# Seven block products in place of eight for four chunk pairs of two gated feed-forward stages

## The chip, the cores and the metric

The kernel runs on one core of one Trainium2 chip. The time is the device time of one execution in microseconds. Before the change it is 990.17 us, the median of three runs (990.16 to 990.27).

## The reference, cut to what matters

Two transformer blocks run on a 256 x 1024 activation `h` in float32. The first block has a gated feed-forward stage, a mixing stage with two kinds of attention, and a second gated feed-forward stage; the second block has attention beside a recurrence, and a squared feed-forward stage. The change touches the two gated stages:

```
def swiglu(x, w_gu, w_down):
    gate, up = jnp.split(x @ w_gu, 2, axis=-1)      # w_gu 1024 x 5632
    return (jax.nn.silu(gate) * up) @ w_down        # w_down 2816 x 1024

h = h + 0.5 * swiglu(rmsnorm(h, ffn1_norm), ffn1_w_gu, ffn1_w_down)
...
h = h + 0.5 * swiglu(rmsnorm(h, ffn2_norm), ffn2_w_gu, ffn2_w_down)
```

## The kernel before, in words

Every large product is made in three passes of fp32r operands. A 128 x 2048 block of weights (four K tiles by 512 columns, 1 MB, called a unit) is loaded by SyncE's queue into one of three buffers `raw`; ScalarE copies it to `hi` (`split_hi`), VectorE subtracts to get `lo` (`split_lo`), and TensorE computes x_hi w_hi + x_hi w_lo + x_lo w_hi. There are three `hi` and three `lo` buffers, so `split_hi` of unit n waits until TensorE has used unit n - 3 (`used` at least n - 2). `portion` is one unit against one tile of 128 tokens: 4 K tiles x 3 passes = 12 matmuls of 128x128 by 128x512. A plain unit is two portions, one for each token tile.

A gated stage is cut into 11 chunks of 256 hidden columns. A chunk's gate and up columns stand side by side in one 512-wide product, whose K = 1024 is two units, so that a chunk is 2 up-projection units (`ffn_up`) and one down-projection unit (`ffn_down`). The order on TensorE is up(i), down(i - 1), in a loop on each engine (`ffn_iter`). The product of chunk i and token tile t goes to PSUM bank `G[t]`. ScalarE takes silu of the left half (`ffn_act`), VectorE multiplies with the right half (`ffn_hidden`), and splits the result's 32-bit words in 16-bit planes (`halves`, `ffn_planes`). SyncE transposes these by DMA (`flip`), VectorE puts the words together (`ffn_merge`), and ScalarE and VectorE split them in `hh` and `hl` (`ffn_hi`, `ffn_lo`) for the down-projection. Its four PSUM banks `DB` gather all chunks. `up(i + 1)` may write `G[t]` only after `ffn_hidden(i, t)` has read it.

The squared stage at the end already has the technique that the change brings to the gated ones: for chunk pairs (2, 3) and (6, 7) the 2 x 2 block product of (two token tiles) by (two chunks) by (two halves of K), eight portions, is made by seven portions on sums of weight blocks (`weight_sum`, VectorE, 128x2048 each), and sums of activation blocks (`x_sums`, `sum_hi`, `sum_lo`, once per stage). Partial results go from PSUM to `xn` (`keep`, ScalarE; `add_product`, VectorE). A product there is a unit that is used by one portion only.

All orders are written out by hand, for each engine a list of calls; every engine works its list strictly in order and waits on counting semaphores. SyncE's queue does this with loads and transposes alike: a load that stands behind a transpose is issued after it.

Of the kernel before, what the change touches and what calls it, by code (L numbers as in the profile page):

```python
# [75 lines left out]

U_F1 = 0
U_M1 = U_F1 + 3 * NF1
U_B1 = U_M1 + 2 * len(IN1)
U_F2 = U_B1 + 8  # L80
U_M2 = U_F2 + 3 * NF1
# [4 lines left out]
PAIRS = (2, 6)  # L86


# [15 lines left out]
OPERAND = {"p1": 0, "p2": 1, "p6": 5, "p7": 2, "p5": 4, "p4": 1, "p3": 3}  # L104
LAST = last_order()
PLAIN = [i for i in range(NF2) if i // 2 * 2 not in PAIRS]
LAST_LOADED = [x for x in LAST if x[0] in "ud"]
UNITS = U_L + len(LAST)

# [6 lines left out]
def slot_of(kind, i, b):  # L116

    return U_L + LAST_LOADED.index((kind, i, b))


def slot_unit(r):

    return r if r < U_L else unit_of(*LAST_LOADED[r - U_L])
# [119 lines left out]
class GatedFfn(Ffn):  # L243


    def __init__(self, sem, name, base, norm, earlier=None):
        super().__init__(sem, name, base, NF1, norm)
        self.past = 0 if earlier is None else NF1
# [8 lines left out]
    def k_tiles(self, i):  # L257

        return 2 if isinstance(i, int) and i == self.chunks - 1 else 0

    def up_unit(self, i):
        return self.base + (0 if i == 0 else 2 + 3 * (i - 1))


class SquaredFfn(Ffn):


    def __init__(self, sem, name, base, norm):
        super().__init__(sem, name, base, NF2, norm)
        self.own(sem, name)  # L270
        self.b_in = [sem(f"{name}_b_in{j}") for j in range(4)]
        self.t_made = sem(name + "_t_made")
        self.s_made = sem(name + "_s_made")
        self.s_hi = sem(name + "_s_hi")
        self.s_lo = sem(name + "_s_lo")
        self.kept = sem(name + "_kept")
        self.added = sem(name + "_added")


def program(nc, a, out):  # L280
    ctx = ExitStack()
    with ctx:
# [40 lines left out]
        with scope() as s:  # L323

            hh = sb("hh", [P, 4, SEQ], F32R, s)
            hl = sb("hl", [P, 4, SEQ], F32R, s)
            halves = sb("halves", [P, NT, 2 * W], U16, s)
            halves_t = sb("halves_t", [P, 8, SEQ], U16, s)
            hid_t = sb("hid_t", [P, 4, SEQ], F32, s)

        with scope() as s:

            operand = {j: sb(f"operand{j}", [P, 4, W], F32, s) for j in (2, 1, 3, 4, 5)}
            sum_h = sb("sum_h", [P, 16, P], F32R, s)
            sum_l = sb("sum_l", [P, 16, P], F32R, s)
# [5 lines left out]
            operand[0] = sb("operand0", [P, 4, W], F32, s)  # L341
# [55 lines left out]

        def whole(n):

            kind, i, b = LAST[n - U_L]  # L400
            return operand[OPERAND[kind]] if kind in OPERAND else raw[slot_of(kind, i, b) % RING]
# [157 lines left out]

        ffns = [GatedFfn(sem, "f1", U_F1, 0)]  # L560
        ffns.append(GatedFfn(sem, "f2", U_F2, 2, ffns[0]))
# [26 lines left out]
        def _(sp_eng):  # L588
            def load(n, src, off=0, dst=None):
                s = n % RING  # L590
                if n >= RING or not isinstance(off, int):

                    sp_eng.wait_ge(lo_done, n - 2 + RING * off)
                sp_eng.dma_start(raw[s][:, :, :] if dst is None else dst(raw[s]), src).then_inc(raw_in[s], UNIT_IN)

            def gate_up(w, n, i, half, off=0):

                s = n % RING
                if n >= RING or not isinstance(off, int):
                    sp_eng.wait_ge(lo_done, n - 2 + RING * off)  # L600
                for g in range(2):
                    src = gu_view(w)[:, bass.ds(i, 1), 4 * half:4 * half + 4, g, :]
# [3 lines left out]
            def columns(w, n, first, half, off=0, width=W):  # L606
                load(n, col_view(w)[:, 4 * half:4 * half + 4, bass.ds(first, width)], off,
                     lambda t: t[:, :, 0:width])

            def down(w, n, i):  # L610
                load(n, down_view(w, 2)[:, i, :, :], 0,
                     lambda t: t[:, :, :].rearrange("p (k h) c -> p k (h c)", h=2))

            def flip(f, i):

                for t in range(NT):
                    sp_eng.wait_ge(f.planes, 2 * i + t + 1)
                    if i > 0:
                        sp_eng.wait_ge(f.merged, i)
                    sp_eng.dma_start_transpose(halves_t[:, 0:4, t * P:(t + 1) * P],  # L620
                                               halves[:, t, 0:W]).then_inc(f.flip[t], 16)

            def last_operand(j, b):

                half, chunk = b % 2, PAIRS[j] + b // 2
                if j == 0:
                    sp_eng.wait_ge(*((k_pv, NH), (k_rl, 2), (k_ri, 8), (k_rl, 2))[b])
                else:
                    sp_eng.wait_ge(lo_done, unit_of(("p1", "p4", "p7", "p3")[b], PAIRS[j - 1]) + 1)
                    sp_eng.wait_ge(last.t_made, 4 * j - (3, 0, 1, 1)[b])  # L630
                src = col_view(a["w_up_2"])[:, 4 * half:4 * half + 4, chunk * W:chunk * W + W]
                sp_eng.dma_start(operand[b][:, :, :], src).then_inc(last.b_in[b], 16)

            def last_load(kind, i, b):

                r = slot_of(kind, i, b)
                sp_eng.wait_ge(lo_done, slot_unit(r - RING) + 1)
                if kind == "u":
                    src = col_view(a["w_up_2"])[:, 4 * b:4 * b + 4, i * W:i * W + W]
                    dst = raw[r % RING][:, :, :]  # L640
                else:
                    src = down_view(a["w_down_2"], 4)[:, i, 2 * b:2 * b + 2, :]
                    dst = raw[r % RING][:, :, :].rearrange("p (k h) c -> p k (h c)", h=2)
                sp_eng.dma_start(dst, src).then_inc(raw_in[r % RING], UNIT_IN)
# [9 lines left out]
            def swiglu_weights(w_gu, w_down, f):  # L654
                gate_up(w_gu, f.base, 0, 0)
                gate_up(w_gu, f.base + 1, 0, 1)
                for i in range(1, NF1):
                    n = f.up_unit(i)
                    if i >= 3:
                        flip(f, i - 2)  # L660
                    gate_up(w_gu, n, i, 0)
                    if i == 2:
                        flip(f, 0)
                    gate_up(w_gu, n + 1, i, 1)
                    down(w_down, n + 2, i - 1)
                flip(f, NF1 - 2)
                down(w_down, f.base + 2 + 3 * (NF1 - 1), NF1 - 1)
# [7 lines left out]
            def slot(n, j):  # L675
# [10 lines left out]
            slot(0, 0)  # L686
            slot(0, 1)
            quarter(1)
            for j in range(2, 4):
                slot(0, j)  # L690
            quarter(2)
            slot(1, 0)
            quarter(3)
            for j in range(1, 4):
                slot(1, j)
            sp_eng.wait_ge(first_hi, 2)
            for j in range(4):
                slot(2, j)
# [13 lines left out]
            down(a["ffn1_w_down"], 4, 0)  # L712
# [10 lines left out]
            part = P // 8  # L723
            for i in range(2, NF1):
                n = ffns[0].up_unit(i)
                if i >= 3:
                    flip(ffns[0], i - 2)
                gate_up(a["ffn1_w_gu"], n, i, 0)
                if i == 2:
                    flip(ffns[0], 0)  # L730

                    sp_eng.wait_ge(ftab_done, 1)
                    sp_eng.wait_ge(pool_made, 1)
                gate_up(a["ffn1_w_gu"], n + 1, i, 1)
                if i < NF1 - 1:
                    sp_eng.dma_start(table[:, (i - 2) * part:(i - 1) * part, :],
                                     ftab[:, :].unsqueeze(1).to_broadcast([24, part, ROW])).then_inc(tab_out, 16)
                down(a["ffn1_w_down"], n + 2, i - 1)
            flip(ffns[0], NF1 - 2)
            down(a["ffn1_w_down"], U_M1 - 1, NF1 - 1)  # L740

# [5 lines left out]
            for c, (first, width, _) in enumerate(IN1):  # L747
                for half in range(2):
                    columns(a["w_in"], U_M1 + 2 * c + half, first, half, width=width)
# [29 lines left out]
            swiglu_weights(a["ffn2_w_gu"], a["ffn2_w_down"], ffns[1])  # L779
# [17 lines left out]
            for c, (first, _) in enumerate(IN2):  # L797
                for half in range(2):
                    if half == 1 and by_dma(c - 3):
                        flip_mixed(c - 3)  # L800
                    columns(a["w_in_2"], U_M2 + 2 * c + half, first, half)
                if c in (3, 6):
# [4 lines left out]
                if c == 12:  # L807
                    last_operand(0, 0)
                if c == 13:
                    last_operand(0, 2)  # L810
# [7 lines left out]
            for c in range(2):  # L818
                for half in range(2):
                    columns(a["w_out_2"], U_P2 + 8 + 2 * c + half, c * W, half)  # L820
                    if half == 1:
                        last_operand(0, (3, 1)[c])
# [12 lines left out]
            last_operand(1, 0)  # L835
# [3 lines left out]
            last_operand(1, 2)  # L839
            last_operand(1, 1)  # L840
            last_load("u", 4, 1)
            flip_last(2, 1)
            last_operand(1, 3)
# [120 lines left out]
        def _(act):  # L964
# [10 lines left out]
            def split_hi(n, off=0, width=W):  # L975
# [3 lines left out]
                act.wait_ge(raw_in[s], UNIT_IN * (n // RING + 1) + UNIT_IN * off)  # L979
                if n >= RING:  # L980

                    act.wait_ge(used, n - 2 + RING * off)
                nc.scalar.activation(hi[s][:, :, 0:width], raw[s][:, :, 0:width], ACT.Copy).then_inc(hi_done, 1)  # L983

            def split_hi_part(n, part):

                s = n % RING
                if part == 0:
                    act.wait_ge(raw_in[s], UNIT_IN * (n // RING + 1))
                    act.wait_ge(used, n - 2)  # L990
                cut = slice(2 * part, 2 * part + 2)
                ins = nc.scalar.activation(hi[s][:, cut, :], raw[s][:, cut, :], ACT.Copy)  # L992
# [1948 lines left out]
```

## Time and profile before

| | |
|---|---|
| median of the runs | 990.17 us |
| the profiled execution | 990.05 us, its span 988.0 us |
| TensorE busy | 981.1 us (99%) |
| VectorE busy | 705.7 us (71%) |
| ScalarE busy | 597.4 us (60%) |
| GpSimd busy | 120.7 us (12%) |
| TensorE's granted clock | full in all but the last slice |

The first gated stage runs from about 7 to 190 us, the second from about 385 to 573 us, and the squared one from about 812 us to the end. A share of busy time is a mean over all stages; for the change the stretch of the gated stages counts. TensorE's matmuls overlap, so a matmul's duration is longer than the distance from one start to the next; the distance is what counts in a row of them.

### The profile page before, as it was taken

The numbers are of one execution on the slowest core, as the hardware profiler recorded it, in microseconds if no ns is written. First come the engines' busy times: TensorE is split into PE (matmuls) and PEld (weight loads), VectorE is DVE, ScalarE is ACT, GpSimd is POOL, SyncE is SP. The second block draws the span as 40 slices with busy tenths as digits, with TensorE's granted clock in tenths as the row PEclk, the third lists the DMA queues.
The fourth block names the chain that finished last, engine by engine and source line by source line (L and its number), as shares of the span: only waits on it lengthen the run. The fifth ranks groups of instructions, "written<-read, shape, count | busy, mean of one in ns | idle before, by whom it ended". The sixth has DMA issues, their size and how long they took to land.

```text
span 988.0 us, 12498 instructions
## 1 busy us (share of the span) xinstructions
PE 981.1 (99%) x4576; PEld 805.1 (81%) x4576; DVE 705.7 (71%) x998; ACT 597.4 (60%) x809; POOL 120.7 (12%) x109
## 2 busy tenths in 40 slices
PE   8999999999999999999999999999999999999998
PEld 6788888888777788888888888888888888888887
DVE  5756565668987667665656677876689878977685
ACT  7344444577666636434444576868876548977772
POOL 0000000022300000000000031249923001000000
PEclk9999999999999999999999999999999999999999
DMA  8987776586544536657575578667665664695542
GB/s 261 284 264 263 229 257 215 170 310 194 167 129 157 184 128 219 214 174 249 170 249 173 188 224 245 176 192 173 217 227 188 238 214 150 201 315 176 188 111 95
DMA packets 167577, 201.96 MB, mean 204 GB/s; under 512 B 58081, under 2 KB 113770, under 8 KB 167402
## 3 DMA queue, kind: packets, MB, share of 16 engines
q1 hardware_dynamic: 166938, 201.21, 64.3%
q8 instruction: 28, 0.46, 0.2%
q10 hardware_dynamic: 592, 0.14, 0.1%
q14 instruction: 19, 0.16, 0.0%
HBM read 182.45 MB, written 5.77 MB: 190 GB/s over the span
## 4 chain that ended last, share of the span: by engine, by line
PE 96%; DVE 2%; ACT 1%; DMA 1%; issue 0%; POOL 0%; SPq 0%; ACTq 0%; DVEq 0%
PE bank L2380 23%; PE bank L2382 23%; PE bank L2381 23%; PE bank L2483 4%; PE bank L2482 4%; PE bank L2481 4%; PE bank L2602 3%; PE bank L2603 3%; PE bank L2601 3%; PE bank L2395 1%; PE bank L2637 1%; PE bank L2752 1%; DMA raw<-in_ffn_w_gu 1%; DVE lo L1626 0%; PE bank L2652 0%
## 5 line engine op out<-in xcount | busy, mean ns | idle before, releaser
L2380 PE MATMUL bank<-hi,xh 128*128 128x512 f32 (+1 forms) x904 | 359.1, 397 | 1.4 <-DVE lo L1981 1.3
L2382 PE MATMUL bank<-hi,xl 128*128 128x512 f32 (+1 forms) x904 | 351.6, 389 | 0.0
L2381 PE MATMUL bank<-lo,xh 128*128 128x512 f32 (+1 forms) x904 | 351.0, 388 | 0.0
L1609 DVE TENSOR_TENSOR lo<-raw,hi 128x2048 fp32r<-128x2048 f32 (+1 forms) x82 | 187.4, 2287 | 94.7 <-ACT hi L983 94.7
L983 ACT ACTIVATE hi<-raw 128x2048 fp32r<-128x2048 f32 (+1 forms) x85 | 161.1, 1898 | 90.9 <-PE bank L2483 57.4
L2380 PEld LDWEIGHTS bank<-hi,xh 128*128 128x128 f32 x904 | 169.8, 188 | 38.7 <-issue 2.1
L2382 PEld LDWEIGHTS bank<-hi,xl 128*128 128x128 f32 x904 | 169.7, 188 | 35.6
L2381 PEld LDWEIGHTS bank<-lo,xh 128*128 128x128 f32 x904 | 170.0, 188 | 32.8
L1626 DVE TENSOR_TENSOR lo<-raw,hi 128x1024 fp32r<-128x1024 f32 (+1 forms) x108 | 131.6, 1228 | 42.6 <-ACT hi L992 41.9
L992 ACT ACTIVATE hi<-raw 128x1024 fp32r<-128x1024 f32 x102 | 104.5, 1051 | 8.9 <-PE bank L2382 8.9
L2481 PE MATMUL bank<-hi,hh 128*128 128x512 f32 x176 | 69.1, 392 | 0.0
L2483 PE MATMUL bank<-hi,hl 128*128 128x512 f32 x176 | 68.6, 390 | 0.0
L2482 PE MATMUL bank<-lo,hh 128*128 128x512 f32 x176 | 68.5, 389 | 0.0
L1767 DVE TENSOR_TENSOR lo<-raw,hi 128x2048 fp32r<-128x2048 f32 x21 | 47.9, 2288 | 19.3 <-ACT hi L1118 19.3
L1051 ACT ACTIVATE act_out<-bank,small 128x256 f32<-128x256 f32 x44 | 20.8, 475 | 56.6 <-PE bank L2382 53.5
L899 POOL TENSOR_TENSOR small<-small 128x1 f32<-128x1 f32 x10 | 8.6, 864 | 371.1 <-DVE small L1633 351.8
L1058 ACT ACTIVATE hh<-hid_t 128x512 fp32r<-128x512 f32 x20 | 12.6, 632 | 66.0 <-DVE hid_t L1671 66.0
L2602 PE MATMUL bank<-lo,last_hh 128*128 128x512 f32 (+1 forms) x130 | 50.1, 386 | 0.0
L2603 PE MATMUL bank<-hi,last_hl 128*128 128x512 f32 (+1 forms) x130 | 50.1, 386 | 0.0
L2601 PE MATMUL bank<-hi,last_hh 128*128 128x512 f32 (+1 forms) x130 | 50.1, 386 | 0.0
L1118 ACT ACTIVATE hi<-raw 128x2048 fp32r<-128x2048 f32 x21 | 40.0, 1914 | 11.8 <-DMA raw<-in_w_down 4.6
L906 POOL TENSOR_TENSOR rstd_q<-ss_q,small 128x8 f32<-128x8 f32 x16 | 34.6, 2169 | 88.4 <-DVE ss_q L2058 88.2
(303 smaller groups left out, 1341.7 us busy)
## 6 DMA issues: line engine op xcount, KB each, us to landing
raw<-in_w_in SPq DMA_DIRECT2D x48, 1024.0 KB
raw<-in_ffn_w_gu SPq DMA_DIRECT2D x82, 512.0 KB
raw<-in_ffn_w_down SPq DMA_DIRECT2D x22, 1024.0 KB
raw<-in_w_down SPq DMA_DIRECT2D x16, 1024.0 KB
raw<-in_w_out SPq DMA_DIRECT2D x8, 1024.0 KB
operand<-in_w_up SPq DMA_DIRECT2D x8, 1024.0 KB, 7.2
raw<-in_w_up SPq DMA_DIRECT2D x8, 1024.0 KB
distance_table<-ftab SPq DMA_DIRECT2D x8, 576.0 KB
```

The costliest lines, as they stand in the source:

```text
L983: nc.scalar.activation(hi[s][:, :, 0:width], raw[s][:, :, 0:width], ACT.Copy).then_inc(hi_done, 1)
L992: ins = nc.scalar.activation(hi[s][:, cut, :], raw[s][:, cut, :], ACT.Copy)
L1609: nc.vector.tensor_tensor(lo[s][:, :, 0:width], raw[s][:, :, 0:width], hi[s][:, :, 0:width].bitcast(F32), ALU.subtract).then_inc(lo_done, 1)
L1626: ins = nc.vector.tensor_tensor(lo[s][:, cut, 0:width], raw[s][:, cut, 0:width], hi[s][:, cut, 0:width].bitcast(F32), ALU.subtract)
L2380: nc.tensor.matmul(o, sh, wh, start=first and j == 0, stop=False, skip_group_check=onto)
L2381: nc.tensor.matmul(o, sh, wl, start=False, stop=False, skip_group_check=onto)
L2382: ins = nc.tensor.matmul(o, sl, wh, start=False, stop=last and j == 3, skip_group_check=onto)
L2481: nc.tensor.matmul(dst, sh, wh, start=first and k == 0, stop=False)
L2482: nc.tensor.matmul(dst, sh, wl, start=False, stop=False)
L2483: ins = nc.tensor.matmul(dst, sl, wh, start=False, stop=end)
L2601: nc.tensor.matmul(dst, sh, wh, start=begin, stop=False)
L2602: nc.tensor.matmul(dst, sh, wl, start=False, stop=False)
```

## The change

In both gated stages the chunks 4 and 5, and 8 and 9, are made by the seven products p1 to p7. The sequence of units of a stage is now a list:

```
FIRST_PAIRS = ((4, 8), (4, 8))
def gated_order(pairs):
    order = [("u", i, u) for i in range(2) for u in range(2)]
    for i in range(2, NF1 - 1, 2):
        d = [("d", i - 2 + c, 0) for c in range(2)]
        if i in pairs:
            p = {k: (k, i, 0) for k in OPERAND}
            order += [p["p1"], p["p2"], p["p6"], d[0], p["p7"], p["p5"], d[1], p["p4"], p["p3"]]
        else:
            order += [("u", i, 0), ("u", i, 1), d[0], ("u", i + 1, 0), ("u", i + 1, 1), d[1]]
    i = NF1 - 1
    return order + [("u", i, 0), ("u", i, 1), ("d", i - 2, 0), ("d", i - 1, 0), ("d", i, 0)]
```

A stage has 39 units in place of 33: 14 of them are products, used by one portion each. A down-projection is now two chunks behind the up-projection. Plain chunks go to banks `G` and `X` in turn, `(G, X)[i % 2][t]`. The loops over chunks are written out, the planes are made by ScalarE (`ffn_planes`), and so are the first three merges. The constants' transposes at the start go to a bank of `DB` in place of `X[1]`.

What a plain chunk waits for on TensorE before its first portion onto a bank:

```diff
-                        if u == 0:
-                            pe.wait_ge(f.hidden, 2 * f.past + 2 * i + t - 1)
-                        ins = portion(n + u, t, G[t], xh, xl, 4 * u, u == 0, u == 1)
+                        if u == 0 and i > 1:
+                            if i - 2 in f.plain:
+                                pe.wait_ge(f.hidden, 2 * f.past + f.order(i - 2, t))
+                            elif i % 2 == 0 and t == 0:
+                                pe.wait_ge(f.hidden, 2 * f.past + f.order(i - 2, 1))
+                            elif i % 2 == 0:
+                                pe.wait_ge(pairs.added, 3 * f.pair(i - 2) + 1)
+                            elif t == 0:
+                                pe.wait_ge(pairs.added, 3 * f.pair(i - 2) + 3)
+                        ins = portion(n, t, (G, X)[i % 2][t], xh, xl, 4 * u, u == 0, u == 1)
```

The results of a pair i, i + 1 stand, for (chunk, token tile): (i, 0) in `c11`, (i, 1) in PSUM bank `G[0]` (p4 is its last product), (i + 1, 0) in `c12`, (i + 1, 1) in `c22`; the c tiles are in `xn`.

The orders of ScalarE and VectorE around a pair (n is the unit of p1, so p2 is n + 1, p6 n + 2, d(i - 2) n + 3, p7 n + 4, p5 n + 5, d(i - 1) n + 6, p4 n + 7, p3 n + 8, up(i + 2) n + 9 and n + 10, d(i) n + 11, and then up(i + 3), or, behind the second pair, d(9) as n + 12 and d(10) as n + 13):

```
ScalarE, gated_pair                      VectorE, gated_pair
split_hi(n + 2)                          weight_sum(j, 3)
keep(j, 0)                               split_lo(n + 2)
split_hi(n + 3)                          if j % 2 == 1: ffn_lo(f, i - 2)
split_hi(n + 4)                          split_lo(n + 3)
keep(j, 1)                               add_product(j, 0)
split_hi(n + 5)                          split_lo(n + 4)
ffn_hi(f, i - 1)                         ffn_merge(f, i - 1)
ffn_act(f, i, 0)                         split_lo(n + 5)
split_hi(n + 6)                          ffn_hidden(f, i, 0)
ffn_planes(f, i, 0)                      weight_sum(j, 4)
keep(j, 2)                               ffn_lo(f, i - 1)
split_hi(n + 7)                          split_lo(n + 6)
split_hi(n + 8)                          split_lo(n + 7)
split_hi(n + 9)                          split_lo(n + 8)
ffn_act(f, i, 1)                         add_product(j, 1)
split_hi(n + 10)                         split_lo(n + 9)
ffn_planes(f, i, 1)                      split_lo(n + 10)
split_hi(n + 11)                         ffn_hidden(f, i, 1)
ffn_act(f, i + 1, 1)                     add_product(j, 2)
ffn_act(f, i + 1, 0)                     split_lo(n + 11)
split_hi(n + 12)                         ffn_hidden(f, i + 1, 1)
ffn_hi(f, i)                             ffn_hidden(f, i + 1, 0)
ffn_planes(f, i + 1, 1)                  ffn_merge(f, i)
ffn_planes(f, i + 1, 0)                  split_lo(n + 12)
ffn_act(f, i + 2, 0)                     ffn_lo(f, i)
ffn_act(f, i + 2, 1)                     ffn_hidden(f, i + 2, 0)
split_hi(n + 13)                         ffn_hidden(f, i + 2, 1)
```

SyncE's queue behind the second pair is, in this order: `flip(f, 8, 0)`, `up(10, 1)`, `dn(8)`, `flip(f, 8, 1)`, `dn(9)`, `dn(10)`, where `dn(i)` is the load of down-projection unit i; behind the first pair the load of up(7)'s first unit stands ahead of `flip(f, 4, 1)`.

## Rows read from the trace of the kernel before

**Rows 1.** The page: TensorE's busy time, and its costliest group.
```profile
PE 981.1 (99%) x4576; PEld 805.1 (81%) x4576; DVE 705.7 (71%) x998; ACT 597.4 (60%) x809; POOL 120.7 (12%) x109
...
L2380 PE MATMUL bank<-hi,xh 128*128 128x512 f32 (+1 forms) x904 | 359.1, 397 | 1.4 <-DVE lo L1981 1.3
```
**Rows 2.** The page: the chain that ended last, by engine.
```profile
PE 96%; DVE 2%; ACT 1%; DMA 1%; issue 0%; POOL 0%; SPq 0%; ACTq 0%; DVEq 0%
```
**Rows 3.** TensorE's waits: who for whom, us in total, times, longest.
```profile
PE bank L2625 <- POOL small L894: 1.8, 1, 1.8
PE bank L2380 <- DVE lo L1981: 1.3, 2, 0.8
PE bank L2637 <- DVE small L1931: 1.1, 1, 1.1
```
**Rows 4.** Busy time in 20 us stretches, then clock, DMA share, GB/s.
```profile
440.00:460.00 20.00, 20.00 (x90) 16.54 (x89) 12.75 (x12) 8.80 (x7) 0.00 (x0) 1.00 0.61 186
...
930.00:950.00 20.00, 20.00 (x90) 16.55 (x89) 17.86 (x12) 14.01 (x14) 0.00 (x0) 1.00 0.30 95
260.00:280.00 20.00, 18.89 (x109) 14.82 (x109) 19.39 (x63) 13.60 (x35) 4.42 (x2) 1.00 0.52 162
```
**Rows 5.** Timeline of ScalarE in the second gated stage's loop: start, duration.
```profile
466.66 1.90 ACT L983 ACTIVATE hi<-raw 128x2048 fp32r<-128x2048 f32 x1
...
472.04 0.48 ACT L1051 ACTIVATE act_out<-bank,small 128x256 f32<-128x256 f32 x1 [2.24 <-PE bank L2382]
472.42 1.91 ACT L983 ACTIVATE hi<-raw 128x2048 fp32r<-128x2048 f32 x1
...
482.98 1.90 ACT L983 ACTIVATE hi<-raw 128x2048 fp32r<-128x2048 f32 x1
```
**Rows 6.** Timeline of TensorE: the first matmul of a down unit.
```profile
471.76 0.39 PE L2481 MATMUL bank<-hi,hh 128*128 128x512 f32 x1
```
**Rows 7.** Timeline of VectorE in the same loop.
```profile
468.59 2.29 DVE L1609 TENSOR_TENSOR lo<-raw,hi 128x2048 fp32r<-128x2048 f32 x1 [1.11 <-ACT hi L983]
470.80 0.48 DVE L1659 SCALAR_TENSOR_TENSOR hid<-bank,small,act_out 128x256 f32<-128x256 f32 x1
...
483.10 0.69 DVE L1677 TENSOR_TENSOR hl<-hid_t,hh 128x512 fp32r<-128x512 f32 x1 [0.80 <-ACT hh L1058]
```
**Rows 8.** The chain at the kernel's start, in order of time.
```profile
8.87 0.70 DVE lo L1981
...
9.71 0.47 PE bank L2380
```
**Rows 9.** Timeline of TensorE around chunk 1's first portion.
```profile
20.07 0.39 PE L2382 MATMUL bank<-hi,xl 128*128 128x512 f32 x1
20.45 0.50 PE L2380 MATMUL bank<-hi,xh 128*128 128x512 f32 x1
20.79 0.39 PE L2381 MATMUL bank<-lo,xh 128*128 128x512 f32 x1
```
**Rows 10.** VectorE's groups by form, 780 to 990 us: count, busy, mean ns.
```profile
L1788 DVE TENSOR_TENSOR operand<-operand 128x2048 f32<-128x2048 f32 x7 | 16.0, 2282 | 0.0
...
L1818 DVE TENSOR_TENSOR xn<-bank,xn 128x512 f32<-128x512 f32 x6 | 4.1, 688 | 1.7 <-PE bank L2382 1.7
```
**Rows 11.** ScalarE's groups by form, the same stretch.
```profile
L1124 ACT ACTIVATE last_halves<-hid 128x1024 uint16<-128x1024 uint16 x8 | 8.5, 1059 | 0.3
...
L1151 ACT ACTIVATE xn<-bank 128x512 f32<-128x512 f32 x6 | 3.6, 592 | 1.8 <-PE bank L2382 1.8
```
**Rows 12.** Timeline of SyncE's queue: issue time and time taken there.
```profile
471.76 2.95 SPq L620 DMA_TRANSPOSE halves_t<-halves  x2
...
481.67 0.40 SPq L594 DMA_DIRECT2D raw<-in_ffn_w_down  x1
```
**Rows 13.** One microsecond of the stretches behind that load.
```profile
486.00:487.00 1.00, 1.00 (x6) 0.81 (x6) 1.00 (x1) 0.12 (x1) 0.00 (x0) 1.00 0.02 8
```
**Rows 14.** Loads of the squared stage's pair operands (L632), 1 MB each.
```profile
DMA to landing us min/median/max: 5.4/7.2/8.6
```

More of the change, by code:

```diff
@@ L255, in __init__, with unit, second, order @@
             self.hh, self.hl, self.d_part = earlier.hh, earlier.hl, earlier.d_part
[L257 to L262, printed above, removed]
+    def unit(self, kind, i, b=0):
+        return self.base + GATED[self.stage].index((kind, i, b))
+    def second(self, i):
+        return i % 2 == 1 and i - 1 in self.pairs
+    def order(self, i, t):
+        return 2 * i + (1 - t if self.second(i) else t) + 1
+    def pair(self, i):
+        return PAIR_AT.index((self.stage, i // 2 * 2))
+    def in_pair(self, i):
+        return i not in self.plain
 class SquaredFfn(Ffn):
@@ L610, in down @@
             def down(w, n, i):
-                load(n, down_view(w, 2)[:, i, :, :], 0,
+                load(n, down_view(w, 2)[:, i, :, :],
                      lambda t: t[:, :, :].rearrange("p (k h) c -> p k (h c)", h=2))
[L614 to L621, printed above, removed]
@@ L721, in _ @@
             sp_eng.dma_start(onehot[:, :], a["onehot"]).then_inc(tab_in, 16)
[L723 to L740, printed above, removed]
+            gated_weights(a["ffn1_w_gu"], a["ffn1_w_down"], ffns[0], table_part)
             def skewed(first, columns_):
@@ new lines, in keep @@
+            def keep(j, k):
+                act.wait_ge(used, pair_unit(j, ("p1", "p6", "p7")[k]) + 1)
+                stage, i = PAIR_AT[j]
+                if k == 0 and i == (FIRST_PAIRS + (PAIRS,))[stage][0]:
+                    act.wait_ge(pairs.s_lo, 4 * stage + 4)
+                elif k == 0 and stage < 2:
+                    act.wait_ge(ffns[stage].hidden, 2 * ffns[stage].past + ffns[stage].order(i - 1, 1))
+                nc.scalar.activation((c11, c12, c22)[k], G[0][:, :], ACT.Copy).then_inc(pairs.kept, 1)
@@ new lines, in ffn_act @@
+            def ffn_act(f, i, t):
+                src = bank_of(f, i, t)
+                if f.in_pair(i):
+                    j = f.pair(i)
+                    if (i % 2, t) == (0, 1):
+                        act.wait_ge(used, pair_unit(j, "p4") + 1)
+                    else:
+                        act.wait_ge(pairs.added, 3 * j + {(0, 0): 1, (1, 1): 2, (1, 0): 3}[i % 2, t])
+                elif t == 0:
+                    act.wait_ge(f.g0, f.g0_past + f.plain.index(i) + 1)
+                else:
+                    act.wait_ge(used, f.unit("u", i, 1) + 1)
+                if i == 0:
@@ L1076, in ffn @@
             def ffn(f, width=lambda n: W):
-                ffn_act(f, 0, 0, f.base + 1)
+                n = f.base
+                one, two = (PAIR_AT.index((f.stage, i)) for i in f.pairs)
+                ffn_act(f, 0, 0)
                 if f.base == 0:
                     half_squares(3)
-                split_hi(f.base + 3)
-                ffn_act(f, 0, 1, f.base + 1)
-                split_hi(f.base + 4)
-                with act.Fori(1, f.chunks - 1) as i:
-                    ffn_iter(f, i, f.base + 2, i - 1)
@@ new lines, in ffn @@
+                ffn_act(f, 1, 0)
+                ffn_act(f, 1, 1)
+                split_hi(n + 6)
+                ffn_hi(f, 0)
+                ffn_planes(f, 1, 0)
+                ffn_planes(f, 1, 1)
+                split_hi(n + 7)
+                for m in (1, 3, 2, 4):
+                    sum_hi(f.stage, m)
+                ffn_act(f, 2, 0)
+                ffn_act(f, 2, 1)
+                split_hi(n + 8)
+                ffn_merge(f, 1)
+                ffn_planes(f, 2, 0)
+                ffn_planes(f, 2, 1)
@@ new lines, in ffn @@
+                split_hi(n + 9)
+                ffn_hi(f, 1)
+                split_hi(n + 10)
+                ffn_merge(f, 2)
+                ffn_act(f, 3, 0)
+                ffn_act(f, 3, 1)
+                split_hi(n + 11)
+                ffn_hi(f, 2)
+                ffn_planes(f, 3, 0)
+                ffn_planes(f, 3, 1)
+                gated_pair(f, one)
+                split_hi(n + 24)
+                ffn_planes(f, 6, 0)
+                ffn_planes(f, 6, 1)
+                ffn_hi(f, 5)
@@ L1800, in x_sums @@
                         (x_block[4], x_block[4], x_block[2], ALU.add))):
+                    if not first <= count < past:
+                        continue
+                    stage = 2 if f is last else f.stage
                     if count > 0:
[L1802 to L1807 removed]
+                        dve.wait_ge(pairs.s_made, 5 * stage + count)
@@ L1820, in last_merge, with add_down @@
+            def add_down(f, t, h):
+                if (t, h) == (1, 1):
+                    dve.wait_ge(used, f.unit("d", NF1 - 1) + 1)
+                else:
+                    dve.wait_ge(f.d_part, f.stage * 3 + 2 * t + h + 1)
+                part = resid[:, t, h * W:(h + 1) * W]
+                nc.vector.scalar_tensor_tensor(part, DB[t][h][:, :], 0.5, part,
+                                               ALU.mult, ALU.add).then_inc(res_done, 1)
             def last_merge(i):
@@ L2477, in ffn_down @@
                         sh, sl = hh[:, kt, rows], hl[:, kt, rows]
                         wh, wl = hi[s][:, 2 * k + h, :], lo[s][:, 2 * k + h, :]
-                        end = last and k == 1
+                        end = final and k == 1
                         dst = DB[t][h][:, :]
-                        nc.tensor.matmul(dst, sh, wh, start=first and k == 0, stop=False)
+                        nc.tensor.matmul(dst, sh, wh, start=i == 0 and k == 0, stop=False)
                         nc.tensor.matmul(dst, sh, wl, start=False, stop=False)
@@ L2542, in product @@
                     if i - 2 in PAIRS:
-                        pe.wait_ge(last.added, 3 * j - 2)
+                        pe.wait_ge(pairs.added, 3 * j - 2)
                     else:
```

993 lines of the change are left out of this document (602 added, 391 removed).

## The prediction

> **What bounds the kernel now.** I read the page's busy times first, then the chain, then TensorE's own waits, then single stretches. TensorE is busy 99% of the span [rows 1], and the chain that ends last is TensorE for 96% [rows 2]. A busy share can hide slow matmuls, so the list of TensorE's waits matters more: all its named waits together are 4.2 us, and none lies inside a gated stage's loop [rows 3]. In the second gated stage 20 us hold 20.00 us of TensorE, and VectorE has 12.75 and ScalarE 8.80 [rows 4]. The gated stages run on matmuls alone. One removed matmul is worth its whole distance, as long as nothing new is late.
>
> **What is removed.** Two `hi` copies that stand at the same place of two turns of the loop start at 466.66 and 482.98, so a chunk takes 16.32 us [rows 5]. It has three units of 24 matmuls: 16.32 / 72 = 0.2267 us a matmul, 2.72 us a portion, 5.44 us a plain unit. A pair needs seven portions in place of eight. Four pairs (two in each stage) save 4 x 2.72 = 10.88 us. A small second saving: chunk 1 no longer waits for chunk 0's bank. In the first stage that bank wait showed as 20.07 to 20.45, 0.38 in place of 0.23 us [rows 9], and the second token tile has its twin 3 us later, so two times 0.15, about 0.3 us. The second stage shows no such wait, so nothing there.
>
> **What is added, off TensorE.** Per stage: six more units to split (1.91 ScalarE, 2.29 VectorE each, [rows 5, 7]), eight weight sums of 2.28, six additions of 0.69 [rows 10], six `keep` of 0.59 [rows 11], and the sums of activations, one of 128x2048 and eight of 128x512, about 2.3 + 8 x 0.69 = 7.8 us. VectorE gets 6 x 2.29 + 18.3 + 4.1 + 7.8 = 44 us. Its load was 12.75 / 20 of a stage of 179.5 us (33 units x 5.44), 114 us; with 44 it is at most 158 of 174 us, 91%, and less, since it gives all plane copies and three merges to ScalarE. The squared stage runs stretches at 17.86 of 20, 89%, with TensorE at 20.00 [rows 4]. So load alone is no bound; what counts is where in the lists a result comes too late. Bytes are the same, so DMA's share (0.61, [rows 4]) stays. The written-out loops cost me nothing: the rest of the kernel is written out too and TensorE stands at 20.00 there (930 to 950); the bound is the 4.2 us of all its waits [rows 3].
>
> **The place that decides: up(i + 2) behind a pair.** Its first portion overwrites `G[0]`, which holds the pair's result (i, 1), finished by p4. So it waits for `ffn_hidden(i, 1)`. On VectorE that call stands behind `split_lo(n + 10)`, which needs `split_hi(n + 10)`, which may not start before p4 has been used. Everything in this chain begins at the end of p4, and TensorE has only p3, one portion, to do meanwhile. From the end of p4:
> - to the start of `ffn_act(i, 1)` 0.28 (TensorE's next unit starts 471.76 [rows 6], ScalarE 472.04 [rows 5]);
> - to the start of `split_hi(n + 10)` 0.38 (472.04 to 472.42);
> - to the start of `split_lo(n + 10)` 1.93 (466.66 to 468.59 [rows 5, 7]);
> - to the start of `ffn_hidden(i, 1)` 2.21 (468.59 to 470.80), and its 0.48;
> - to TensorE 0.14 (VectorE ends at 8.87 + 0.70 = 9.57, the matmul starts at 9.71 [rows 8]).
>
> Sum 5.42 us. p3 covers 2.72. TensorE stands for 2.70, and the first matmul after a stop costs 0.34 in place of 0.23 to the next one (20.45 to 20.79 [rows 9]), 0.11 more: 2.81 us a pair, 4 x 2.81 = 11.2 us. This is as large as what is saved. Bounds: if `split_hi` were to start at once and the hand-overs were free, 1.90 + 2.29 + 0.48 - 2.72 = 1.95 us a pair; with VectorE held by `split_lo(n + 9)` half a microsecond longer, 3.3. I take the chain's value, as each link is a row of the same kind of instruction. Queued behind the waiting matmul is all of TensorE's work.
>
> **Smaller places.** (a) d(i - 1), unit n + 6. From the end of p1: `keep` starts 0.20 later (at least; 0.28 above), `split_hi(n + 3)` about 0.5 later, `split_lo(n + 3)` 1.93 later; then VectorE has lo, add, lo, merge, lo, hidden, weight sum, `ffn_lo`, lo back to back, with starts 0.08 closer than the durations (468.59 + 2.29 against 470.80): 4 x 2.29 + 2.28 + 0.69 + 0.75 (a merge, estimated from 128x1024 words of 16 bits at the rate of its neighbours) + 0.48 + 0.69 - 0.6 = 13.4, in all 16.0 and 0.14 to TensorE, of the 6 x 2.72 = 16.3 us until d(i - 1). On the edge: 0 to 0.5, I take 0.05 a pair, 0.2. (b) d(8) behind the second pair. The plane copy after `ffn_hidden(8, 1)` takes about 0.63 (half of 1.06 [rows 11] and a fixed part), the flip then holds SyncE for about 1.25, and only then is d(9)'s load issued: about 5.42 - 0.14 + 0.13 + 0.63 + 0.1 + 1.25 = 7.4 after p4. A 1 MB load of this kind issued at 481.67 [rows 12] has no traffic left at 486.0 [rows 13], 4.2 to 4.3; with a flip just ahead in the rings I take 4.6. So `split_hi(n + 12)` starts at 12.1, `split_lo(n + 12)` at 14.0, `ffn_lo(8)` at 16.25, its end 16.94, TensorE 17.1. d(8) was due at 2.72 + 2.81 + 10.88 = 16.4: 0.7 and 0.1 to restart, 0.8 a stage, 1.6. Behind the first pair the load stands ahead of the flip, so `ffn_lo(4)` waits for TensorE's own late up unit and comes just in time (0). (c) d(9) needs flips that are issued about when d(8) starts: 0 to 0.5, I take 0.1 a stage, 0.2.
>
> **The sum**, against the profiled execution's 990.05: - 10.88 - 0.3 + 11.2 + 0.2 + 1.6 + 0.2 = + 2.0, so 992.1. The median of the runs is 0.12 above the profiled one; the small places could each be nothing. I say 992.0.
>
> **A rule against the change.** At 260 to 280 us TensorE once stands for over a microsecond and the granted clock stays 1.00, its upper level, 2.4 GHz [rows 4]. The new stops are twice as long and more, and no row has one such. The Trainium skill, TensorE: Matmul & The Clock Gate, section Why this matters for your kernels, tells to have no long idle gaps of the array between bursts, since the clock falls to the lower level. If it did, matmuls would be 0.453 us apart for a while; at a portion after each of four stops that is + 10.9 us, rival 3.
>
> **Rivals.**
> 1. *The saving comes through*, TensorE does not stand at `G[0]`. For it: in the squared stage the same seven products run with TensorE at 20.00 [rows 4]. Against it: the chain begins at p4 by the code and 1.95 us is its floor. With neither (b): 990.05 - 11.2 + 0.4 = 979.3. If only a part of the stops is there, some 984 to 988.
> 2. *d(9)'s load lands late* (slower). One mechanism: SyncE issues it behind `flip(8, 1)`, and ScalarE's `split_hi(n + 12)` stands ahead of `ffn_hi(8)`, so that d(8) waits for the load of d(9). It decides from a landing of 3.9 us on; the squared stage's operand loads took 7.2 in the median, up to 8.6 [rows 14]. At 7.2 it costs 2.6 a stage more than I took: 992.0 + 5.2 = 997.2; at 8.6, 1000. Against it: the load is alone with one flip there, and rows 12 and 13 show such a one.
> 3. *The clock falls after the stops*: 1003.
>
> **How the numbers follow.** Forecast 0.66, its own range 988.5 to 995 (four stops of 1.95 to 3.3 us, and 0 to 5 us from (a) to (c)). Rival 1 0.15 (0.09 whole, 0.06 in part), rival 2 0.15, rival 3 0.04. This kernel's measurement can tell about 0.2%, 2 us, from no change: 988.2 to 992.15. The forecast lies at the edge of it; I give 0.41 of its 0.66 to within and 0.23 to slower, 0.02 to faster. Faster 0.17, same 0.41, slower 0.42. The range 987 to 998 leaves out the whole saving (0.09), a part of rival 1, rival 3 and late landings over 7.5 us.
>
> **What the changed profile would show.** TensorE's waits would have up(6)'s and up(10)'s first matmuls, released by VectorE's `hid`, four times 2.7 us, where the list was empty before. In the windows the gated pairs would show TensorE short of 20 by as much. VectorE's `hid` there would start 2.2 us behind a `lo`. A wait of d(8) for `hl` with ScalarE's `hi` released by the DMA of w_down would show (b). I am wrong if the up units follow p3 without a gap, or if a wait of over a microsecond stands elsewhere.

## The result: 996.9 us, slower, and the profile after

The changed kernel takes 996.88 us (median of 4 runs, 995.64 to 998.33) against 990.22 us (990.16 to 990.40) before. The ratio is 1.0067, 95% interval 1.0050 to 1.0085. The profiled execution took 998.33 us, the longest of the four, with a span of 996.5 us, 8.5 us over that of before. The time of this kernel spreads over 2.7 us from run to run, that of before over 0.2 us here, and over 1.3 us in the 19 executions of before that stand beside the first experiments. Each execution also has a mean granted clock of TensorE: 0.995 for three of the four here, 0.996 for the fastest; it is 1.0 for all executions of before that stand beside the experiments.

TensorE's list of waits in the trace of after, to be read against [rows 3] (who for whom, us in total, times, longest):

```profile
PE bank L2650 <- DVE hid L1930: 9.9, 4, 2.5
PE bank L2803 <- DVE hl L1946: 2.8, 3, 1.3
PE bank L2945 <- POOL small L1020: 1.8, 1, 1.8
PE bank L2957 <- DVE small L2201: 1.1, 1, 1.1
PE bank L2650 <- DVE lo L2251: 0.5, 2, 0.2
```

The first two rows are new. `hid` is `ffn_hidden(i, 1)`, four times, once behind each pair; `hl` is the operand of a down-projection. Around the first pair of the first stage, the timeline of TensorE shows the stop and what comes behind it (start, duration):

```profile
93.82 0.39 PE L2650 MATMUL bank<-hi,first_sum_h 128*128 128x512 f32 x1
...
96.31 0.39 PE L2652 MATMUL bank<-hi,first_sum_l 128*128 128x512 f32 x1
99.17 0.47 PE L2650 MATMUL bank<-hi,xh 128*128 128x512 f32 x1 [2.46 <-DVE hid L1930]
99.47 0.40 PE L2651 MATMUL bank<-lo,xh 128*128 128x512 f32 x1
...
100.43 0.63 PE L2652 MATMUL bank<-hi,xl 128*128 128x512 f32 x1
100.86 0.63 PE L2650 MATMUL bank<-hi,xh 128*128 128x512 f32 x1
...
102.99 0.63 PE L2652 MATMUL bank<-hi,xl 128*128 128x512 f32 x1
103.42 0.56 PE L2650 MATMUL bank<-hi,xh 128*128 128x512 f32 x1
103.81 0.39 PE L2651 MATMUL bank<-lo,xh 128*128 128x512 f32 x1
```

p3's first matmul starts at 93.82 and its last at 96.31, up(6)'s first at 99.17: 2.85 us between starts in place of 0.23, a stop of 2.62 us. (Below, a stop is always this distance less 0.23.) From 100.43 to 103.42 the matmuls start 0.427 us apart in place of 0.227. The window rows give the granted clock (third number from the end) for this stretch, and for those behind the third and the fourth pair:

```profile
101.00:103.00 2.00, 2.00 (x7) 1.52 (x6) 1.48 (x1) 1.28 (x3) 0.00 (x0) 0.50 0.69 117
...
477.00:479.00 2.00, 2.00 (x6) 1.60 (x5) 0.69 (x1) 2.00 (x3) 0.00 (x0) 0.50 0.33 78
...
544.00:546.00 2.00, 2.00 (x6) 1.58 (x5) 0.85 (x1) 1.91 (x3) 0.00 (x0) 0.52 0.50 64
```

0.50 is the lower level, 1.2 GHz. TensorE had stood for 2.6 us before each. In these stretches TensorE is "busy" all the time, 2.00 of 2.00: the busy share doesn't show this loss, the distance of the starts and the count (x7 or x6 in 2 us, where some 9 are due) do. Behind the second pair the same stop was not followed by a fall.

What makes `hid` late is seen in VectorE's timeline at the same place:

```profile
93.31 2.29 DVE L1820 TENSOR_TENSOR lo<-raw,hi 128x2048 fp32r<-128x2048 f32 x1 [2.54 <-ACT hi L1114]
96.33 2.29 DVE L1820 TENSOR_TENSOR lo<-raw,hi 128x2048 fp32r<-128x2048 f32 x1 [0.73 <-ACT hi L1114]
98.54 0.48 DVE L1930 SCALAR_TENSOR_TENSOR hid<-bank,small,act_out 128x256 f32<-128x256 f32 x1
```

`split_lo(n + 10)` waits 0.73 us for `hi`, runs 2.21 us, then `hid` runs and ends at 99.02; TensorE starts 0.15 later. VectorE's own idle time there is 0.73 us: a full engine is not what makes it late. The silu had been ready since 94.49, in ScalarE's timeline:

```profile
94.02 0.47 ACT L1205 ACTIVATE act_out<-bank,small 128x256 f32<-128x256 f32 x1 [0.74 <-PE bank L2652]
94.39 1.91 ACT L1114 ACTIVATE hi<-raw 128x2048 fp32r<-128x2048 f32 x1
```

**The balance of the profiled execution.** Removed: 10.88 us. Added: four stops of 2.85 - 0.23 = 2.62, and 0.08 each to restart (0.31 in place of 0.23), 10.8; d(8), 1.67 and 1.03 us between matmuls, with the restarts 2.4; d(0) of the first stage, 1.27, 1.1; three stretches at the lower clock, each about seven matmuls 0.200 us longer and some 0.15 at its ends, about 1.55 each, 4.6. Sum 18.9 - 10.9 = 8.0 of the 8.5 us.

### The profile page after: what moved, and what is told of

Same layout as the page of the kernel before. It is cut to its first block, busy times and chain, and to the rows that moved or that the text cites. A ratio compares the mean times of both kernels' runs of the same rounds, so it can differ in the third digit from the quotient of the medians.

```text
span 996.5 us, 12257 instructions
## 1 busy us (share of the span) xinstructions
PE 977.5 (98%) x4528; PEld 799.9 (80%) x4528; DVE 765.9 (77%) x1010; ACT 657.9 (66%) x887; POOL 118.9 (12%) x109
## 4 chain that ended last, share of the span: by engine, by line
PE 89%; DVE 3%; DMA 2%; issue 2%; ACT 2%; SPq 1%; POOL 0%; ACTq 0%; DVEq 0%; POOLq 0%
PE bank L2650 21%; PE bank L2652 21%; PE bank L2651 21%; PE bank L2803 4%; PE bank L2805 4%; PE bank L2804 4%; PE bank L2922 3%; PE bank L2921 3%; PE bank L2923 3%; PE bank L2665 1%; DMA raw<-in_ffn_w_down 1%; PE bank L2957 1%; ACT hi L1114 1%; DMA halves_t<-halves 1%; PE bank L3072 1%
## 5 line engine op out<-in xcount | busy, mean ns | idle before, releaser
L2650 PE MATMUL bank<-hi,xh 128*128 128x512 f32 (+1 forms) x824 | 330.7, 401 | 10.6 <-DVE hid L1930 9.9
L2652 PE MATMUL bank<-hi,xl 128*128 128x512 f32 (+1 forms) x824 | 322.6, 391 | 0.0
L2651 PE MATMUL bank<-lo,xh 128*128 128x512 f32 (+1 forms) x824 | 321.7, 390 | 0.0
L2650 PEld LDWEIGHTS bank<-hi,xh 128*128 128x128 f32 x824 | 156.1, 189 | 46.0 <-DVE lo L1820 11.4
L2652 PEld LDWEIGHTS bank<-hi,xl 128*128 128x128 f32 x824 | 155.8, 189 | 33.2
L2651 PEld LDWEIGHTS bank<-lo,xh 128*128 128x128 f32 x824 | 156.4, 190 | 30.0
L1820 DVE TENSOR_TENSOR lo<-first_operand,hi 128x2048 fp32r<-128x2048 f32 x28 | 64.1, 2288 | 4.6 <-ACT hi L1114 4.5
L1114 ACT ACTIVATE hi<-first_operand 128x2048 fp32r<-128x2048 f32 x28 | 53.6, 1916 | 18.8 <-PE bank L2652 12.9
L2803 PEld LDWEIGHTS bank<-hi,hh 128*128 128x128 f32 x176 | 33.0, 188 | 10.5 <-DVE lo L1820 2.7
L1820 DVE TENSOR_TENSOR lo<-last_operand,hi 128x2048 fp32r<-128x2048 f32 x14 | 32.0, 2287 | 9.1 <-ACT hi L1114 9.1
```

Of the source, the lines that this page charges most:

```text
L1114: nc.scalar.activation(hi[s][:, :, 0:width], whole(n)[:, :, 0:width], ACT.Copy).then_inc(hi_done, 1)
L1820: nc.vector.tensor_tensor(lo[s][:, :, 0:width], whole(n)[:, :, 0:width], hi[s][:, :, 0:width].bitcast(F32), ALU.subtract).then_inc(lo_done, 1)
L2650: nc.tensor.matmul(o, sh, wh, start=first and j == 0, stop=False, skip_group_check=onto)
L2651: nc.tensor.matmul(o, sh, wl, start=False, stop=False, skip_group_check=onto)
L2652: ins = nc.tensor.matmul(o, sl, wh, start=False, stop=last and j == 3, skip_group_check=onto)
L2803: nc.tensor.matmul(dst, sh, wh, start=i == 0 and k == 0, stop=False)
```

## The experiments

All ratios are against the kernel before; the medians are of 4 to 10 runs.

### VectorE: hidden ahead of split_lo

```diff
+                ffn_hidden(f, i, 1)
                 split_lo(n + 10)
-                ffn_hidden(f, i, 1)
                 add_product(j, 2)
```

> Only VectorE's list differs: ffn_hidden(i, 1) stands ahead of split_lo(n + 10). Theory (bank wait plus clock): the four stops at the first matmul of up(6) and up(10), 2.85 us each in the trace of after, vanish, since hidden(i, 1) now ends about 2.2 us after p4 and p3 covers 2.72; with them goes the time at half clock behind them (5.1 us). 996.9 - 10.7 - 5.1 = 981 us; d(8)'s stop stays near 0.5 to 1.5 a stage. Rival A (VectorE is simply full, the lateness moves to another place): stops of 2 us turn up at d(4) and d(8), 988 to 992. Rival B (the clock fell for another reason than the stops): the granted clock still shows 0.5 behind the pairs, 986.

Measured 983.51 us (982.86 to 986.25), ratio 0.9936 (0.9919 to 0.9953), 13.4 us less than after. TensorE's waits:

```profile
PE bank L2803 <- DVE hl L1946: 3.1, 4, 1.3
...
PE bank L2650 <- DVE lo L2251: 0.8, 2, 0.6
```

Nothing waits for `hid`. This trace holds no record of the granted clock (its page has no PEclk row), so the 1.0 that is listed for this execution says nothing; the starts of the matmuls do. Behind the first pair, in the stretch from up(6)'s first matmul on:

```profile
97.22 0.39 PE L2650 MATMUL bank<-hi,xh 128*128 128x512 f32 x1
...
100.84 0.39 PE L2651 MATMUL bank<-lo,xh 128*128 128x512 f32 x1
```

These are 16 distances of 0.226 us, and nowhere in the trace do four matmuls in a row start over 0.38 us apart. What is left is four stops for `hl`: 1.44 (d(0)), 0.55 (d(4), first stage) and 0.75 and 1.02 (d(8)), together 3.8 with no restarts counted; 983.5 - 3.8 is 979.7, the pure saving. d(4)'s stop is new, since up(6) no longer comes late and so no longer covers it. The time is 2.5 us above the expected 981. Of that 0.5 are the falls, which the expectation counted at 5.1 us and which cost 4.6, and 0.6 the stops for `hl`, together longer than in after by that; the rest is open. Rival A holds for half a microsecond of its 7 to 11. Rival B falls for the profiled execution; another of the four, the one of 986.25 us, has a mean clock of 0.998, so a fall can still come here, and where it came isn't known.

### TensorE: useless matmuls in the stop

```diff
                             elif i % 2 == 0 and t == 0:
+                                pe.wait_ge(pairs.added, 3 * f.pair(i - 2) + 1)
+                                for _ in range(11):
+                                    nc.tensor.matmul(G[1][:, :], xh[:, 0, 0:P], xh[:, 0:2, :].rearrange("p k c -> p (k c)"),
+                                                     start=True, stop=True)
                                 pe.wait_ge(f.hidden, 2 * f.past + f.order(i - 2, 1))
```

> TensorE makes 11 matmuls of 128x512 onto the free bank G[1], whose values are overwritten, during the wait for hidden(i, 1) (11 x 0.227 = 2.5 us). Nothing else differs from after. Theory: the wait lasts as long, but TensorE isn't idle, so that the clock stays at its upper level and the 5.1 us at half clock are saved: 996.9 - 5.1 = 991.8. Rival B (the clock falls for another reason): 996.9 and clock 0.5 still shown.

Measured 993.52 us (992.47 to 994.38), ratio 1.0031 (1.0021 to 1.0040), 3.4 us less than after though it makes 44 more matmuls. TensorE in the stretch of the first pair, its timeline and then the windows:

```profile
96.49 2.65 PE L2738 MATMUL bank<-xh 128*128 128x512 f32 x11
99.02 0.50 PE L2650 MATMUL bank<-hi,xh 128*128 128x512 f32 x1
99.36 0.39 PE L2651 MATMUL bank<-lo,xh 128*128 128x512 f32 x1
...
103.47 0.39 PE L2651 MATMUL bank<-lo,xh 128*128 128x512 f32 x1
```

```profile
98.00:100.00 2.00, 2.00 (x10) 1.45 (x9) 1.56 (x3) 1.00 (x2) 0.00 (x0) 1.00 1.05 350
100.00:102.00 2.00, 2.00 (x10) 1.63 (x10) 0.53 (x1) 2.00 (x3) 0.00 (x0) 1.00 0.94 211
```

This trace too has no record of the clock, so the 1.00 in its windows is no evidence. The starts are: from 99.36 to 103.47 they are 0.228 us apart where after had 0.427, ten in 2 us in place of seven, and behind none of the four pairs is there a slow stretch. The products and operands are those of after, and `hid` is as late (it starts at 98.48, in after at 98.54), so the fall comes from TensorE's idling.

The saving is 3.4 and not 5.1. The 5.1 is half of the time that the clock was low in after's profile; counted by matmuls three falls cost 4.6. Three of after's four executions have the mean clock of three falls, 0.995, so 996.9 - 4.6 = 992.3 was due. Of the other 1.2 us, 1.0 is seen: d(8)'s stops were longer (2.20 and 1.46 us between matmuls in the profile, in after 1.67 and 1.03), as d(8) is due earlier while the load that it waits for isn't.

### SyncE: the load of down unit 9 ahead of the flip

```diff
+                dn(9)
                 flip(f, 8, 1)
-                dn(9)
```

> Only SyncE's list differs: the load of down unit 9 is issued ahead of flip(8, 1), as up(7)'s is behind the first pair. Theory: the load of d(9) lands long before split_hi(n + 12) wants it, ScalarE's wait for the DMA (4.3 and 5.3 us in after) vanishes and with it the stops of d(8), 1.44 and 0.80 us and their restart: 996.9 - 2.4 = 994.5. The four bank stops and the half clock remain. Rival (d(8) is late by VectorE's list whatever the load): 996.9.

Measured 993.68 us (991.58 to 994.19), ratio 1.0031 (1.0021 to 1.0041), 3.2 us less than after. ScalarE's copy `hi` of unit 9 behind the second pair, after first and then this kernel:

```profile
173.51 1.92 ACT L1114 ACTIVATE hi<-raw 128x2048 fp32r<-128x2048 f32 x1 [4.32 <-DMA raw<-in_ffn_w_down]
```

```profile
169.06 1.92 ACT L1114 ACTIVATE hi<-raw 128x2048 fp32r<-128x2048 f32 x1 [2.70 <-PE bank L2652]
```

It now waits for its buffer (TensorE) and not for the DMA, and TensorE's list has no `hl` row at all:

```profile
PE bank L2650 <- DVE hid L1930: 9.9, 4, 2.5
PE bank L2945 <- POOL small L1020: 1.8, 1, 1.8
PE bank L2957 <- DVE small L2201: 1.1, 1, 1.1
PE bank L2650 <- DVE lo L2251: 0.7, 2, 0.5
```

d(8)'s stops came from the load. d(0)'s stop is missing as well, which this edit doesn't touch; that stop comes and goes from one execution to the next. The clock fell behind one of the four bank stops here, behind three in after, with the same length of stop (2.85 us between starts in all eight). So the saving isn't the load's alone: the two profiled executions differ by 6.4 us, and 2.4 (d(8)), 1.1 (d(0)) and 3.1 (two falls) make 6.6. The ten executions of this kernel have mean clocks of 0.998 and 0.997, less of the lower clock than after's 0.995 and 0.996, and the medians' 3.2 us hold a part of that.

### SyncE: nothing beside that load

```diff
                 flip(f, 8, 1)
                 dn(9)
+                r = slot(f.unit("d", 9))
+                sp_eng.wait_ge(raw_in[r % RING], UNIT_IN * (r // RING + 1))
```

> SyncE waits for the landing of down unit 9 before it issues the loads behind it (down unit 10 and the next stage's first one). In after it landed 5.65 us after its issue, where I had taken 4.6. Theory (it shares the rings with down unit 10's load, issued 0.5 us behind it): alone it lands in 4.3 to 4.6 us, and d(8)'s stops shrink by about 1 us each in both stages: 996.9 - 1.9 = 995. Rival (the flip ahead of it makes it late): 5.5 us again and 996.9.

Measured 1000.22 us (997.50 to 1001.49), ratio 1.0105 (1.0088 to 1.0122). My theory falls. SyncE's timeline and ScalarE's release by the load:

```profile
166.20 5.78 SPq L659 DMA_DIRECT2D raw<-in_ffn_w_down  x2
```

```profile
171.59 1.92 ACT L1116 ACTIVATE hi<-raw 128x2048 fp32r<-128x2048 f32 x1 [4.06 <-DMA raw<-in_ffn_w_down]
```

Alone the load takes 171.59 - 166.20 = 5.4 us, against 173.51 - 167.86 = 5.65 beside the next one, which in after is issued right behind it:

```profile
167.86 1.11 SPq L659 DMA_DIRECT2D raw<-in_ffn_w_down  x2
```

The windows of the stretch with the load alone show the last of its traffic in 170 to 171 us, and then 0.6 us until ScalarE starts at 171.59:

```profile
170.00:171.00 1.00, 1.00 (x6) 0.84 (x5) 0.51 (x1) 0.00 (x0) 0.00 (x0) 1.00 0.61 250
171.00:172.00 1.00, 1.00 (x7) 0.81 (x6) 0.00 (x0) 0.41 (x1) 0.00 (x0) 1.00 0.01 4
```

So my 4.2 to 4.3 from [rows 12, 13] was the end of the traffic, not the release of the engine that waits. In the second stage the load took 5.2 us alone and 5.4 beside the next one; so the neighbour is worth some 0.2 us and not 1. Whether the flip ahead adds to the rest wasn't tried. The kernel got slower since down unit 10's load now came late: d(9) had stops of 1.21 us in the first stage and 1.97 in the second, and d(8) still had 1.21 and 1.72. The profiled execution is the fastest of the four, with one fall; the others have mean clocks of 0.995 to 0.997, more falls, and the median is theirs.

### VectorE: half of the stop, and a longer one

```diff
-                split_lo(n + 10)
+                split_lo_part(n + 10, 0)
                 ffn_hidden(f, i, 1)
+                split_lo_part(n + 10, 1)
```

> In VectorE's list split_lo(n + 10) is made in two halves, and ffn_hidden(i, 1) stands between them. Theory: hidden comes 2.21 - 1.15 = about 1.1 us earlier, so the four stops are 1.5 us in place of 2.6 (gaps of 1.8 between matmuls in place of 2.85). before has a stop of 1.5 us at 260 us with the clock at 1.00, so the clock stays up: 996.9 - 4 x 1.1 - 5.1 = 987.4, with d(8)'s stops perhaps 1 us longer since d(8) comes earlier. Rival (any stop at this place brings the clock down): 992.5.

```diff
                 split_lo(n + 10)
+                nc.vector.tensor_tensor(c21, resid[:, 0, 0:W], resid[:, 0, 0:W], ALU.add)
                 ffn_hidden(f, i, 1)
```

> A useless addition of 128x512 (0.69 us, starts 0.61 apart) stands ahead of ffn_hidden(i, 1) on VectorE. Theory: gaps of 3.45 us in place of 2.85, four times 0.6 more, and the clock falls behind all four stops in every run, in place of some of them: 996.9 + 2.4 + about 1.7 = 1001. d(8)'s stop gets no longer (its load is later by the same 0.6). Rival (the clock's falls don't depend on the stop's length): 999.3.

Half of it: 989.76 us (988.61 to 992.61), ratio 0.9998 (0.9988 to 1.0007). Longer: 999.74 us (999.18 to 1000.66), ratio 1.0095 (1.0079 to 1.0112). TensorE's first wait, half and then longer:

```profile
PE bank L2651 <- DVE hid L1930: 5.6, 4, 1.4
```

```profile
PE bank L2651 <- DVE hid L1930: 12.3, 4, 3.1
```

Between matmuls these are 1.78 and 3.45 us, stops of 1.56 and 3.23 us. In the profiled executions, the clock stays at 1.00 behind all four with half the stop, and it is at the lower level behind all four with the longer one. Behind the second pair, where after showed no fall:

```profile
168.00:170.00 2.00, 2.00 (x6) 1.58 (x5) 0.75 (x1) 2.00 (x3) 0.00 (x0) 0.50 0.51 82
```

The stop in the profile is dosed as expected, and the clock follows it, but not in every execution, as I had expected. The mean clocks of the longer one's four are 0.993, 0.993, 0.995 and 0.997 (a profiled execution with four falls has 0.993, with three 0.995, with one 0.998), so two had fewer than four falls. Of the halved kernel's ten executions two have 0.998, one fall each, though in its profile no stop is over 1.62 us. Behind which stop they came isn't known. Longer stops make the fall more frequent; a length below which it never comes isn't shown.

The halved kernel lies 2.4 us above what I expected: its d(8) had stops of 1.62 and 1.50 us, 0.9 more than in after, since the load is on its own time, and the falls were counted at 5.1 in place of 4.6; the rest is open. The longer one lies 1.3 us under: fewer falls than expected in two of its executions, and d(8) had no stop in the first stage and 0.43 us in the second, 1.8 less than in after, as it is due later while its load isn't.

### The two, and all three

The third edit, beside those of the first and third experiment:

```diff
-                if f.base == 0:
-                    x_sums(f, 1, 5)
                 ffn_lo(f, 0)
+                if f.base == 0:
+                    x_sums(f, 1, 5)
```

> hidden(i, 1) first and the load of down unit 9 first, without the change at d(0). Theory: what is left to the version with all three is d(0)'s stop alone, 1.0 to 1.3 us in the first stage: 979.3 + 1.2 = 980.5. Rival (the d(0) step is worth nothing, as other waits would take its place): 979.3.

> hidden(i, 1) first, the load of down unit 9 first, and in the first stage ffn_lo(0) ahead of the four small activation sums (d(0) stood 1.27 us for it in after). Theory: only TensorE's work remains, 990.2 - 10.9 = 979.3, at most 1 us more; TensorE's list of waits has nothing from the gated stages. Rival A (VectorE full): 982 or more, with waits for hl.

The two: 979.63 us (979.31 to 980.89), ratio 0.9897 (0.9881 to 0.9914). All three: 979.27 us (979.04 to 980.32), ratio 0.9890 (0.9874 to 0.9907). Between them lies 0.4 us and not 1.2, within what the runs spread; d(0)'s stop was not in the profiled execution of the two. Its length goes with what ScalarE's in-order list waits for DMA just ahead of it, for a load and then for chunk 0's flips: 7.4 us with `hidden` ahead (stop 1.44), 6.9 in after (1.04), 6.0 in the two (none) and 4.4 with only the load moved (none). Why these land later in one execution than in another is open. With all three, TensorE's list of waits has nothing from the gated stages, and the second stage's two pairs run full:

```profile
PE bank L2945 <- POOL small L1020: 1.8, 1, 1.8
PE bank L2957 <- DVE small L2201: 1.1, 1, 1.1
PE bank L2650 <- DVE lo L2251: 0.9, 2, 0.6
```

```profile
460.00:480.00 20.00, 20.00 (x90) 16.54 (x89) 16.07 (x14) 11.85 (x15) 0.00 (x0) 1.00 0.91 271
540.00:560.00 20.00, 20.00 (x96) 16.10 (x95) 12.74 (x20) 10.69 (x18) 0.00 (x0) 1.00 0.47 150
```

This version beats both kernels: 990.2 - 979.3 = 10.9 us, as much as the removed 48 matmuls (10.88). The weight sums, the additions and the six more units per stage cost nothing that can be seen in the time, at VectorE 16.07 of 20.

## Why the prediction was right, and where it was not

The place and the size of the main loss were as predicted, and so was the direction, which the prediction gave as good as even chances (slower 0.42, same 0.41). The forecast was 992.0, the measured time 996.9, inside the range, 5 us off. That it lies inside is partly luck. The upper part of the range was made of longer bank stops, small places and late loads, and the falls of the clock, which the range left out, make 4.6 of the 8.5 us. Against the forecast's + 2.0 the profiled execution has 4.6 more by the clock, 1.1 by d(0), 0.8 by d(8) and 0.3 since chunk 1's saving isn't seen in it, 0.4 less by the four stops and 0.4 less by the other small places: + 8.0 of the 8.5.

- *The saving*: 10.88 forecast, 10.9 measured in the version without the stops. Right.
- *The stop at G[0]*: 2.70 us and 0.11 to restart forecast, 2.62 and 0.08 measured, four times. Each link of the chain holds; only the distance from the end of p4 to the silu is 0.08 shorter than I had it (p3's first matmul at 93.82, the silu at 94.02: 0.20 in place of 0.28). The experiment that moves one call takes the whole stop away.
- *The clock*: here the prediction failed. "At 260 to 280 us TensorE once stands for over a microsecond and the granted clock stays 1.00", and I made the fall rival 3, at 0.04, as if forecast and fall excluded each other. The fall happened on top of the forecast. It cost 4.6 us in the profiled execution, 1.55 a fall, and not the 2.7 of rival 3: about seven matmuls were slow, not a portion of twelve, at 0.427 us and not 0.453. The row of before has a stop of 1.5 us; mine were 2.6, so the row bore nothing out for them. The profiled execution with stops of 1.56 us agrees with it, the one with stops of 3.23 us has four falls of four. The Trainium skill (TensorE: Matmul & The Clock Gate, Why this matters for your kernels), on which rival 3 drew, warns of long idle gaps between bursts of matmuls. The trace agrees: 0.50 in the windows above, behind stops of 2.62 us.
- *d(8)*: forecast 0.8 a stage, measured 1.44 and 0.80 and the restarts, 2.4 in place of 1.6. The mis-sized term is the landing, 4.6 forecast, 5.65 measured in the first stage and 5.37 in the second: I had read the end of traffic for the release. Rival 2 was the right mechanism for this part at 5.65 in place of 7.2; that d(8) waits for the load of d(9) is shown.
- *d(0)*, 1.1 us in the first stage, I had not looked at; its stop of about a microsecond is what the prediction named at its end as a sign of being wrong, a wait elsewhere. ScalarE's list has the load of up(2) and the flips in it, and four small sums stand ahead of `ffn_lo(0)` on VectorE.
- *d(i - 1)* and *d(9)*: forecast 0.2 each, no stop seen in after. *Chunk 1's bank wait*: the 0.3 us may have been saved, but the first matmuls of this execution came later by as much; it can't be told apart.
- *Rival 1* fell for this kernel; its time, 979.3, is what the version with three moved calls reaches.

## What to carry to other kernels

When fewer products stand between the last write of a PSUM bank and its next use, follow the reader of that bank through its engine's whole list: a long instruction that stands ahead of it and that itself begins at the same event is not hidden by anything. A stop costs its length and, the more often the longer it is, also the clock behind it; here a stop of 2.62 us cost some 1.55 us more whenever the clock fell. And a product saved at one engine is only worth something if the calls around it are put in order anew; here three moved lines separate +0.7% from -1.1%.

## What the runs showed of the hardware that I had not expected

- In the profiled executions, stops of TensorE of 2.62 us were followed by the lower clock in 3 of 4 places (after) and in 1 of 4 in each of two others (the two kernels with only SyncE's list changed), stops of 3.23 us in 4 of 4, and no stop of up to 1.97 us by any. In executions that weren't profiled the clock also fell in two kernels whose profiles show no stop over 1.62 us, as the mean clock of each execution tells:

| kernel | executions, us, by their mean clock |
|---|---|
| after | 995.64 at 0.996; 996.83 to 998.33 at 0.995 (three) |
| load of down unit 9 first | 991.58 to 993.28 at 0.998 (four); 993.67 to 994.19 at 0.997 (six) |
| nothing beside that load | 997.50 at 0.998; 1000.36 at 0.997; 1000.09 and 1001.49 at 0.995 |
| half of the stop | 988.61 to 990.89 at 1.0 (eight); 990.67 and 992.61 at 0.998 |
| longer stop | 999.20 at 0.997; 999.18 at 0.995; 1000.28 and 1000.66 at 0.993 |
| `hidden` ahead | 982.86 to 983.66 at 1.0 (three, the profiled one without a record of the clock); 986.25 at 0.998 |

The versions with two and with three edits have 1.0 in all eight executions.

- The count of falls moves the time of one program. In the second row the two groups lie 1.6 us apart in the mean, about the 1.55 us of a fall counted by matmuls. It isn't all of the spread: the eight executions of the halved kernel at 1.0 spread over 2.3 us, the one with all three edits over 1.3 us.
- The lower clock can show some time behind the stop, when the matmuls have already begun again (99.17, then 100.43, in the first stage), or before they do. Behind the third pair TensorE's first matmul starts at 475.96, and the clock has already fallen:

```profile
475.00:476.00 1.00, 0.04 (x1) 0.07 (x1) 1.00 (x3) 0.15 (x1) 0.00 (x0) 0.91 0.98 327
```

- A 1 MB load releases the waiting ScalarE 5.1 to 5.65 us after its issue. In the one followed by windows its traffic was over at most 4.8 us after the issue, and ScalarE started at 5.4.
